# Routed experts: the down weights of a pair are asked for on the scalar engine's queue

## The reference

```
def swiglu(x, w_gate, w_up, w_down):
    return (jax.nn.silu(x @ w_gate) * (x @ w_up)) @ w_down
...
    def body(acc, bidx):
        rows = lax.dynamic_slice_in_dim(tok_buf, bidx * MOE_ROW_BLOCK, MOE_ROW_BLOCK)
        wr = lax.dynamic_slice_in_dim(w_buf, bidx * MOE_ROW_BLOCK, MOE_ROW_BLOCK)
        e = blk_expert[bidx]
        ye = swiglu(xt[rows], w_gate_e[e], w_up_e[e], w_down_e[e]) * wr[:, None]
        return acc.at[rows].add(ye.astype(acc.dtype)), None
```

## Time and profile before

| what | before |
|---|---|
| median of 3 runs | 1454.57 us (1452.04 to 1466.34) |
| the profiled execution | 1460.52 us, span 1458.7 us |
| TensorE busy | 1323.3 us, 91% of the span |
| ScalarE busy | 476.8 us, 33% |
| VectorE busy | 551.6 us, 38% |
| chain that ended last | PE 85%, DVE 6%, DMA 4% |
| moved by SyncE's queue (q1) | 365.29 MB |
| moved by ScalarE's queue (q10) | 2.94 MB |
| routed experts, from the first gate/up matmul to the last scatter | 327 to 866 us |

### The profile page before, as it was taken

How to read it: one execution, slowest core, us unless ns; L and a number is a source line. 1 busy time by engine, 2 the same in 40 slices (tenths; PEclk the granted TensorE clock), 3 DMA queues, 4 the chain that set the end, 5 groups by cost and what they waited for, 6 DMA issues and landing times.

```text
span 1458.7 us, 16861 instructions
## 1 busy us (share of the span) xinstructions
PE 1323.3 (91%) x6656; PEld 908.8 (62%) x6656; DVE 551.6 (38%) x735; ACT 476.8 (33%) x692; POOL 30.5 (2%) x41
## 2 busy tenths in 40 slices
PE   3799998779999999999999977999969978599996
PEld 0777777664544554454454436888859767488885
DVE  0545456643111111111111125464544653554543
ACT  1354444322222122222222224434333633434342
POOL 1000000000000000000000000030000000000000
PEclk9899999789999999999999998999989969899999
DMA  9976755568999999999999995655614204355640
GB/s 353 355 274 234 246 181 176 201 248 346 392 380 399 393 398 385 409 393 384 376 370 383 384 324 144 211 183 173 217 38 156 97 1 156 105 176 200 201 142 29
DMA packets 133529, 372.32 MB, mean 255 GB/s; under 512 B 14771, under 2 KB 62180, under 8 KB 118316
## 3 DMA queue, kind: packets, MB, share of 16 engines
q1 hardware_dynamic: 131824, 365.29, 68.5%
q10 hardware_dynamic: 1340, 2.94, 0.6%
q0 software_dynamic: 320, 3.46, 0.6%
HBM read 368.47 MB, written 4.50 MB: 256 GB/s over the span
## 4 chain that ended last, share of the span: by engine, by line
PE 85%; DVE 6%; DMA 4%; ACT 2%; issue 1%; SPq 1%; POOL 1%; POOLq 0%; ACTq 0%; DVEq 0%
PE bank L1780 28%; PE bank L1941 15%; PE bank L1873 9%; PE bank L1965 8%; PE bank L1913 4%; PE bank L1977 4%; PE bank L1834 4%; DMA ada_g<-in_w_ada 2%; DMA ring<-in_w_up_e 2%; DVE h_tok L1147 1%; PE bank L2030 1%; PE bank L2054 1%; PE bank L1796 1%; PE bank L1767 1%; PE bank L1930 1%
## 5 line engine op out<-in xcount | busy, mean ns | idle before, releaser
L1941 PE MATMUL bank<-ring,xg 128*64 128x512 f32 x1088 | 248.5, 598 | 3.4 <-DMA ring<-in_w_up_e 3.3
L1132 DVE TENSOR_TENSOR g_lo<-raw_g,g_hi 128x2048 fp32r<-128x2048 f32 (+2 forms) x88 | 201.8, 2294 | 125.8 <-ACT g_hi L723 66.3
L1780 PE MATMUL bank<-g_hi,xt_hi 128*128 128x512 f32 (+1 forms) x592 | 240.1, 406 | 4.7 <-DVE arena L1177 2.5
L1780 PE MATMUL bank<-g_hi,xt_lo 128*128 128x512 f32 (+1 forms) x592 | 233.0, 394 | 0.0
L1780 PE MATMUL bank<-g_lo,xt_hi 128*128 128x512 f32 (+1 forms) x592 | 232.3, 392 | 0.0
L1941 PEld LDWEIGHTS bank<-ring,xg 128*64 128x64 f32 x1088 | 79.4, 137 | 141.9 <-issue 133.6
L1780 PEld LDWEIGHTS bank<-g_hi,xt_hi 128*128 128x128 f32 x592 | 113.4, 192 | 33.5 <-issue 7.3
L1780 PEld LDWEIGHTS bank<-g_hi,xt_lo 128*128 128x128 f32 x592 | 112.5, 190 | 24.0
L1965 PE MATMUL bank<-ring,a_t 128*64 128x512 f32 x544 | 124.2, 598 | 3.4 <-ACT a_t L824 1.3
L1780 PEld LDWEIGHTS bank<-g_lo,xt_hi 128*128 128x128 f32 x592 | 113.3, 191 | 21.9
L1271 DVE SCALAR_TENSOR_TENSOR arena<-arena,w_row_of,bank 128x256 f32<-128x256 f32 x34 | 16.3, 480 | 242.4 <-ACT arena L820 242.4
(11 more groups left out here) (294 smaller groups left out, 1712.9 us busy)
## 6 DMA issues: line engine op xcount, KB each, us to landing
ring<-in_w_up_e SPq DMA_DIRECT2D x64, 1024.0 KB, 19.7
ring<-in_w_gate_e SPq DMA_DIRECT2D x64, 1024.0 KB, 10.8
ring<-in_w_down_e SPq DMA_DIRECT2D x32, 2048.0 KB, 18.2
raw_g<-in_ffn_w_gu SPq DMA_DIRECT2D x44, 1024.0 KB, 9.2
raw_g<-in_w_in SPq DMA_DIRECT2D x26, 1024.0 KB, 7.1
raw_d<-in_ffn_w_down SPq DMA_DIRECT2D x22, 1024.0 KB, 5.0
ada_d<-in_w_ada SPq DMA_DIRECT2D x16, 1024.0 KB, 5.1
raw_g<-in_w_out SPq DMA_DIRECT2D x8, 1024.0 KB, 5.0
```

Of the source, the lines that this page charges most:

```text
L1132: dve.tensor_tensor(lo, raw, hi.bitcast(F32), ALU.subtract).then_inc(S.lo_g, 1)
L1780: last = pe.matmul(out_, src[s][:, c, b * P:(b + 1) * P], w((g_hi, g_lo)[m], i), start=start and i == 0 and k == 0, stop=stop and i == len ...
L1941: last = pe.matmul(bank(4)[r, :].rearrange("p (g n) -> p g n", g=2), xg[:, s // 2 % 2, c, at_:at_ + ROWS], gate_up_raw(s, j, c), start=c = ...
```

## The change

The down weights of pairs 2 to 31 are no longer asked for by SyncE but by ScalarE. In SyncE's `load_pair` the wait on `y_ps` and the down transfer go. In ScalarE's `body(s)` the same transfer for pair s + 1 is issued behind the two `y_hi` copies of pair s - 1, for s from 1 to 30; the second of these copies has waited for all of that pair's `y_ps`, so that no wait is added. Destination, size and semaphore of the transfer are the same. Pairs 0 and 1 and the spare pairs keep their down transfers on SyncE.

```
@@ SyncE, load_pair
                 sp.wait_ge(used_gu, at(4 * (s - 2) + 2 * u + 2, it, 16))
                 for g in range(2):
                     load_half(s, u, g, it)
-            sp.wait_ge(y_ps, at(4 * (s - 1), it, 16))
-            load_rows_down(s, it)
@@ ScalarE, sparse_phase
+                def load_rows_down(s, it=None):
+                    first = at(2 * s, it, 8)
+                    src = a["w_down_e"][0][first:first + 2] if it is None else a["w_down_e"][0][bass.ds(first, 2)]
+                    dst = ring[:, s % 2, 4 * UNIT:6 * UNIT].rearrange("p (e n) -> p e n", e=2)
+                    act.dma_start(dst, src.rearrange("e (p c) n -> p e (c n)", c=2)).then_inc(landed_dn[s % 2], 16)
+
                 def body(s, it=None):
                     more = s + 2 < N_PAIR or it is not None
                     if s:
                         rows_down(s - 1, it)
+                    if 1 <= s < E // 2 - 1:
+                        load_rows_down(s + 1, it)
                     if more:
                         gathered(2 * s + 4, it)
```

## The result

The changed kernel took 1451.61 us, median of 20 runs (1449.85 to 1454.41), the kernel before 1460.03 us beside it, also median of 20 (1452.04 to 1466.94). The ratio is 0.9939, with a 95% interval of 0.9923 to 0.9955: 8.4 us faster, 4.9 us under the predicted 1456.5. It is within 1% and within the range, but it moved the other way than the +2 us forecast, and clear of the scatter. What also changed is the scatter itself, from 15 us to 5.

What follows compares the result with a forecast made beforehand. It took TensorE and the DMA engines both to be full, the DMA a little short. Terms 0 + 0 + 0 + 2 = +2 us on the three-run median of 1454.57 gave 1456.5 us, range 1447 to 1470.

Steps and rivals of the forecast that it cites:

- +2 us forecast: Routed experts: one more group of slow matmuls after an early wait, 1.6 us rounded to +2 us; all other terms 0.
- ScalarE's issue cost nothing: ScalarE, between second y_hi copy and silu: 30 down issues of 0.45 us each, with 7.0 us of cover, cost 0.
- The 0 us that the prediction drew from the rule: DMA queues: spreading transfers over issuing engines doesn't help bandwidth, so by this alone the change is worth 0.
- The slowest engine needs 15.75 + 0.58 = 16.3 us for its share of a pair: Routed experts' DMA: halves age 0.58 us more each pair, so the slowest DMA engine needs 16.3 us against TensorE's 15.75.
- its last byte comes at the same moment in whatever order the earlier ones came: Slowest DMA engine, routed experts: its backlog never breaks, so reordering transfers leaves its end time unchanged.
- The halves were to be 25.7 us old: Gate/up halves mid-stage: down transfers put ahead raise their age from 20.4 to 25.7 us, with 28.1 allowed.
- the first wait was to come near 690 us: TensorE in the routed experts: its first wait on weights comes just after 690 us instead of at 757.
- 5.4 us is all that the DMA costs before: Three late pairs of routed experts take 52.67 us, not 47.25, so waits cost 5.4 us, bounding any gain.
- (c): Rival, SyncE's queue: no longer full, rate back to 397 GB/s, waits vanish, -5.4 us, 1449; chance 0.20.
- (b): Rival, from pair 2 on: turns between two queues slow the slowest engine, 16.8 us a pair, +15 us, 1470; chance 0.17.
- (d): Rival, ScalarE: held in its issue up to 8.07 us, in the last 10 pairs, +11 us, 1465; chance 0.07.
- (a): Rival, the forecast itself: TensorE's waits come earlier but sum to the same, time within a few us; chance 0.56.

Runs made afterwards that it cites:

- both kernels where the DMA sets the pace: Half of the gate/up matmuls left out, in the kernel before and in the changed one: 1422.29 us with one queue, 1427.45 us with two.

## Why the prediction was wrong

**What held.** SyncE's wait hid nothing. ScalarE's issue cost nothing: 0.38 us in a gap of 4 us, at most 0.42 in the stage. The down weights land after 11.9 us; 8 to 12 was said. The two queues take turns, and the down overtakes the halves. One or two engines do fall behind. The +2 us of the sum did not come: they were one more group of slow matmuls after a wait, and there was no wait. That the time came within 4.9 us of the forecast is luck: the kernel before was 5.5 us slower by its twenty runs than by the three shown, and the gain of 8.4 us took that back and more. The Trainium skill's rule that spreading over issuing engines brings no bandwidth ("DMA: Bandwidth & Descriptors", section "Rules for kernel authors") agrees with the 414 GB/s of both kernels where the DMA sets the pace. The 0 us that the prediction drew from the rule did not come out: without more rate the kernel became 8.4 us faster.

**What failed first** is the sentence "The slowest engine needs 15.75 + 0.58 = 16.3 us for its share of a pair". I read a growing age as a fixed rate. One queue moves a pair in 15.2 us when all engines have work, and the same program ages differently in three executions. The rows themselves spoke against a fixed rate: from 20.4 to 24.1 us in some nine pairs is 0.4 us a pair, not 0.58, and the growth up to 16 or 18 us is there in the changed kernel too. What the runs show in its place is a lag that depends on how the bytes are asked for: it grows with large transfers in one queue, and not with a second queue or with all of 512 KB. With it goes "its last byte comes at the same moment in whatever order the earlier ones came". The halves were to be 25.7 us old and were 18.2; the first wait was to come near 690 us and none came.

**What failed second** is a size: "5.4 us is all that the DMA costs before". That was the cost in one execution. The floor of the stage with the old wait value is 530.8 to 531.0 us in seven profiles of six kernels, one of them a profile of the kernel before itself. The kernel before was at 530.9, 534.9 and 536.1 us, in executions of 1450.5, 1455.0 and 1460.5 us. Its times reach from 1449 to 1479 us over all jobs, those of the changed kernel from 1449 to 1455, so the median gain of 8.4 us passes the bound that I had set for a gain. In the two profiled executions the stage gained 5.1 us, close to the bound. The 5.5 us that they differ by after the stage are the clock.

**The rivals.** (c), with 0.20, had the outcome: no wait on the ring, a bound of 1449. It had the wrong reason. The queue with one stream is full from early on in the kernel where the DMA sets the pace, and moves 414 GB/s; and in the kernel before the lag came first and the long issues after it: by 558 us the last four signals of a half had fallen from 1.3 to 3.9 us behind, while no issue of SyncE in the stage had taken over 0.53 us; the first long one, 1.09 us, is at 572. (The row of 0.37 us at 610.48 is not typical of its time: two issues near it, at 598.80 and 603.53, took 1.16 and 1.33 us.) (b) and (d) did not occur: neither did the rate fall nor was ScalarE held. The order of chances among (a), (b) and (c) was set by one profile; the three times shown, 1452 to 1466, could have told that something in this kernel varies. No wait on the ring at all was also the sign that it had named.

**What stays open.** Why one or two engines drift away from the rest with large transfers in one queue, and why by another amount in each execution. Shown is that each of four things leaves a profile without a wait on the ring: a second queue on ScalarE or GpSimd, with half or all of the down weights or with half of gate/up; two down transfers; gate/up transfers of 512 KB; all of 512 KB. Only the two down transfers with 8 KB rows still had some long executions. No profile caught an execution of the kernel before above 1461 us. That its long executions are waits on the ring is inferred: the clock is ruled out, the two profiles with a lag of 7 us have such waits, and whatever ends the waits in the profile ends nearly all of the scatter.

## What to carry to other kernels

Where a stream of weights keeps the DMA engines nearly full, read the age of the transfers at several places, and compare the landing of the first sixteen signals with the last: if they drift apart, cut the transfers (512 KB here) or use a second queue, before you believe in a lack of bandwidth. A bound on a gain that comes from the waits of one profile is a bound for that execution alone; take a second profile when the times shown scatter more than the forecast moves. Compare times with the granted clock beside them: what the clock does not explain is the kernel's. Where wait values are worked out in a loop, try to make them equal; here 1.5 to 1.7 us came with it.

## What the hardware showed that I had not expected

With the DMA setting the pace, one queue and two move the same 414 GB/s, but with TensorE asking for only 399 or 390 GB/s one or two engines fall back in one queue, to an age of 24 us. Asking for twelve transfers in place of five for the same 6 MB held nothing up, though two issues take SyncE some 0.85 us, about 5 us in a pair's 15.75. It brought a half from 20.4 us to between 12.0 and 12.7. And with equal wait values on TensorE's queue some 0.1 us went in every other pair, 1.5 to 1.7 us in the stage.
